# A sixth modulation unit folded by VectorE in the first FFN, and none left to the first attention

## The reference

```python
def adaln(cond, w, b):
    m = jax.nn.silu(cond) @ w + b
    return [t[:, None, :] for t in jnp.split(m, N_MOD, axis=-1)]

def ffn_sublayer(x, shift, scale, gate, g_pre, g_post, w_in, w_out):
    h = modulate(rmsnorm(x, g_pre), shift, scale)
    a, b = jnp.split(h @ w_in, 2, axis=-1)
    h = (jax.nn.silu(a) * b) @ w_out
    return x + FFN_RES * gate * rmsnorm(h, g_post)
```

## Time and profile before

| | |
|---|---|
| median of three runs | 3013.35 us (3012.11 to 3014.33) |
| the profiled execution's own time | 3015.84 us |
| its span | 3014.0 us, 46617 instructions |
| TensorE busy | 98% |
| VectorE busy | 73% |
| ScalarE busy | 38% |
| GpSimd busy | 19% |
| DMA | 517.76 MB, mean 172 GB/s |
| chain that ended last | TensorE 89% |

### The profile page before, as it was taken

One profiled execution on the slowest core, in us unless ns is written; L12 is line 12 of the kernel. 1 busy time (PEld: TensorE's weight loads), 2 busy tenths in 40 slices (PEclk: granted clock), 3 DMA queues, 4 the chain that ended last, 5 costly groups with the idle time before them and its releaser, 6 DMA issues.

```text
span 3014.0 us, 46617 instructions
## 1 busy us (share of the span) xinstructions
PE 2957.3 (98%) x18194; PEld 2748.1 (91%) x18194; DVE 2207.0 (73%) x2897; ACT 1153.1 (38%) x1966; POOL 564.2 (19%) x586
## 2 busy tenths in 40 slices
PE   7999999999999999999999999999999999999999
PEld 6999888999999998999899999979999999889998
DVE  6888678887987656888888576768888888775444
ACT  4222664223322424222422365543224222664222
POOL 1111212112111212111211144631112111211001
PEclk9999999999999999999999999999999999999999
DMA  8667436665665445766566443337665666333443
GB/s 299 210 213 216 146 84 193 211 211 170 215 213 175 116 131 173 226 211 197 185 214 192 134 118 105 97 95 236 211 209 184 216 211 200 108 81 113 127 128 96
DMA packets 589696, 517.76 MB, mean 172 GB/s; under 512 B 66773, under 2 KB 523046, under 8 KB 587686
## 3 DMA queue, kind: packets, MB, share of 16 engines
q1 hardware_dynamic: 588918, 514.53, 56.6%
q10 hardware_dynamic: 560, 0.25, 0.0%
HBM read 510.37 MB, written 4.33 MB: 171 GB/s over the span
## 4 chain that ended last, share of the span: by engine, by line
PE 89%; issue 4%; DVE 2%; POOL 2%; ACT 1%; DMA 1%; SPq 0%; another core or an unknown queue 0%; DVEq 0%; POOLq 0%; ACTq 0%
PE bank L1698 19%; PE bank L1700 18%; PE bank L1699 18%; PE bank L1749 9%; PE bank L1748 9%; PE bank L1747 9%; PE bank L1715 2%; PE bank L1722 1%; PE bank L619 1%; PE bank L644 1%; DMA ada_first<-w_ada 1%; PE bank L1780 0%; POOL small L2379 0%; POOL small L2384 0%; POOL hg_kr L1497 0%
## 5 line engine op out<-in xcount | busy, mean ns | idle before, releaser
L1698 PE MATMUL bank<-h_hi,w_hi 128*128 128x384 f32 x3328 | 1120.7, 337 | 0.0
L1700 PE MATMUL bank<-h_hi,w_lo 128*128 128x384 f32 x3328 | 1114.6, 335 | 0.0
L1699 PE MATMUL bank<-h_lo,w_hi 128*128 128x384 f32 x3328 | 1113.7, 335 | 0.0
L1934 ACT ACTIVATE w_hi<-raw 128x1024 fp32r<-128x1024 f32 x646 | 680.6, 1062 | 1022.8 <-PE bank L1700 481.8
L2090 DVE TENSOR_TENSOR w_lo<-raw,w_hi 128x1024 fp32r<-128x1024 f32 x648 | 811.1, 1275 | 310.6 <-ACT w_hi L1934 305.4
L1698 PEld LDWEIGHTS bank<-h_hi,w_hi 128*128 128x128 f32 x3328 | 625.3, 188 | 11.0 <-ACT tmp L1953 1.6
L1699 PEld LDWEIGHTS bank<-h_lo,w_hi 128*128 128x128 f32 x3328 | 625.4, 188 | 6.1
L1700 PEld LDWEIGHTS bank<-h_hi,w_lo 128*128 128x128 f32 x3328 | 625.1, 188 | 0.0
L2117 DVE SCALAR_TENSOR_TENSOR fold<-ada_raw,cond,fold 128x1024 f32<-128x1024 f32 x462 | 616.4, 1390 | 0.1
L2420 POOL TENSOR_TENSOR h_lo<-tmp,h_hi 128x384 fp32r<-128x384 f32 x176 | 249.3, 1416 | 1758.7 <-DVE h_hi L2161 1758.7
L1749 PE MATMUL bank<-w_hi,h_lo 128*128 128x512 f32 x1056 | 414.0, 392 | 0.0
(11 more groups left out here) (204 smaller groups left out, 2445.9 us busy)
## 6 DMA issues: line engine op xcount, KB each, us to landing
raw<-w_ffn_in SPq DMA_DIRECT2D x352, 512.0 KB, 5.0
ada_raw<-w_ada SPq DMA_DIRECT2D x264, 512.0 KB, 4.2
raw<-w_ffn_out SPq DMA_DIRECT2D x176, 512.0 KB, 4.7
raw<-w_hgrn_in SPq DMA_DIRECT2D x40, 512.0 KB, 4.1
g_rows<-g_dram SPq DMA_DIRECT2D x12, 1024.0 KB, 7.0
raw<-w_attn_qkv SPq DMA_DIRECT2D x24, 512.0 KB, 5.4
raw<-w_conv_in SPq DMA_DIRECT2D x24, 512.0 KB, 5.0
ada_first<-w_ada SPq DMA_DIRECT2D x16, 512.0 KB, 10.5
```

The lines of the kernel that those rows point to most:

```text
L1698: mm(out, wh, h_hi[:, k, :], start=(k == 0), stop=False)
L1699: mm(out, wh, h_lo[:, k, :], start=False, stop=False)
L1700: last = mm(out, wl, h_hi[:, k, :], start=False, stop=(k == DC - 1))
L1934: A(w_hi[:, b % RING, :], raw[:, b % RAW, :], ACT.Copy).then_inc(w_hi_made, 1)
```

## The change

The first FFN makes units 2 to 7, the first attention none. An FFN with up to five units keeps one in four iterations; the one with six has them start at f = 0, 4, 8, 11, 15, 18, so that three of them have three iterations, with three, three and two slabs. Their sums come at f = 4, 8, 11, 15, 18, 21, and the unit that is left over to the attention is unit 7 instead of unit 6. In SyncE's queue the slabs of the first FFN stand from block at_a(f) + 5 on, not + 3.

```diff
-    units_of = {0: (2, 7), 1: (7, 8), 2: (8, 13), 3: (13, 17), 4: (17, 17), 5: (17, 22), 6: (22, 26), 7: (26, 26),
+    units_of = {0: (2, 8), 1: (8, 8), 2: (8, 13), 3: (13, 17), 4: (17, 17), 5: (17, 22), 6: (22, 26), 7: (26, 26),
                 8: (26, 31), 9: (31, 36), 10: (36, 36), 11: (36, 36)}
     units_end = [units_of[s][1] for s in range(12)]
-    FOLD_F = 4
+    UNIT_STARTS = {5: (0, 4, 8, 12, 16, 20), 6: (0, 4, 8, 11, 15, 18, 21)}
+
+    def unit_starts(s):
+
+        u0, u1 = units_of[s]
+        return UNIT_STARTS[max(u1 - u0, 5)]
 
     def sums_of(s):
 
         u0, u1 = units_of[s]
-        return {FOLD_F * (u - u0 + 1): u for u in range(u0, u1)}
+        return {unit_starts(s)[u - u0 + 1]: u for u in range(u0, u1)}
...
-        u0, u1 = units_of[s]
-        u = u0 + f // FOLD_F
-        return [(u, 2 * (f % FOLD_F) + n) for n in range(2)] if u < u1 else []
+        starts = unit_starts(s)
+        for i, u in enumerate(range(*units_of[s])):
+            length = starts[i + 1] - starts[i]
+            if starts[i] <= f < starts[i + 1]:
+                per = -(-DC // length)
+                first = per * (f - starts[i])
+                return [(u, k) for k in range(first, min(first + per, DC))]
+        return []
...
-                        slabs.setdefault(at_a(f) + 3 + n, []).append(slab)
+                        slabs.setdefault(at_a(f) + (5 if s == 0 else 3) + n, []).append(slab)
```

## The result

The changed kernel took 3020.27 us in the median of 20 runs (3015.05 to 3026.24), the kernel before 3013.47 us beside it (20 runs, 3011.65 to 3017.41). The ratio, taken between runs made side by side, is 1.0018 with a 95% interval of 1.0012 to 1.0025, which is +5.4 us (+3.6 to +7.5). The forecast was −1.45 us, so it missed in size and in sign. The 3013.35 us that the forecast started from, plus 5.4, is 3018.8 us, above its range of 3008.7 to 3015.2. The profiled execution took 3020.82 us, with a span of 3019.0.

The account below looks back on a forecast made before the run. The prediction took TensorE, busy 98% of the span, as the bound. It summed −4.2 us in the attention and +2.75 us in the first FFN to −1.45 us, taking the median from 3013.35 to about 3011.9 us, range 3008.7 to 3015.2.

Parts of the forecast that it names:

- The attention, −4.2 us: First attention, up to its first scores: without its unit it takes the second attention's 21.76 us, saving 4.2 us.
- Steady part, three-slab iterations: First FFN, f = 8 to 19: VectorE lags 0.57 us, makes it up, and TensorE loses nothing.
- VectorE's work in the tail: End of first FFN: product 19 at 282.3, intervals 11.1 and 9.1 us, TensorE waits 2.0 us, boundary starts at 306.8.
- SyncE's queue … Cost nothing: First FFN's load queue: slabs loaded two blocks later still come ahead of their folds, at no cost.
- The term for the first FFN: End of first FFN: the added slabs and sums start VectorE's boundary chain late, +2.75 us.
- Rival D: First FFN's tail: last slab or unit 6's parts come late through SyncE's queue; +1.55 us, 3014.9; chance 0.08.
- The rule on the clock: First boundary: gaps between matmul bursts halve TensorE's clock, so the tail's new wait could add 1.7 us.
- rival C: First boundary gets a half-clock stretch, or another moves onto a boundary: +1.7 us, at most 3013.6; chance 0.13.
- a tail of 2.75 us: End of first FFN: the sixth unit's extra VectorE work delays the boundary by 2.75 us.

Follow-up runs that it names:

- packed version: Changed kernel with the first FFN's gains written as 128 rows of 64 bytes, layout left wrong: 3012.09 us, ratio 0.9994.
- second changed execution: The changed kernel profiled once more, unaltered: 3015.46 us.
- write from ScalarE: Changed kernel with the first FFN's scattered gains write issued from ScalarE's queue behind the Silu of f = 19: 3019.97 us, ratio 1.0018.
- write ahead of the slabs: Changed kernel with the first FFN's gains write directly behind block 63's load, before the two slabs there: 3018.65 us, ratio 1.0018.
- gains earlier: Changed kernel with the first FFN's gains write issued at block 61 instead of block 63: 3016.42 us, ratio 1.0008.
- third changed execution: The changed kernel profiled another time, unaltered: 3021.96 us.
- second of the kernel before: The kernel before the change profiled once more, unaltered: 3011.54 us.
- earlier starts: Changed kernel with the first FFN's units started at f = 0, 4, 7, 10, 13, 16 and ended at 19: 3010.37 us, ratio 0.9987.

## Why the prediction was wrong, point by point

- **The attention, −4.2 us: right.** The control in the same trace gave 21.76 us and 21.75 came; over three executions, taken from low parts to the next sublayer's low parts, the term is −3.7.
- **Steady part, three-slab iterations: right.** The lag was 0.4 us where I had 0.57, and it was made up.
- **VectorE's work in the tail: right.** Product 19 came at 282.15 (282.3). The packed version shows the intervals of 11.1 and 9.0 us, TensorE's wait of 2.0 us (in the changed kernel it does not come, since TensorE is held up earlier), and the boundary with next to no idle time (0.20 us).
- **"SyncE's queue … Cost nothing": this step failed.** I moved the slabs by two blocks and looked at what that does to slabs and weight loads in the steady part. I did not list what else stands in the queue at the last blocks. The write of the gains at block 63 was moved past by two slab loads, which wait for folds, so it left at 279.22 and not at 268.31, and the load behind it landed so late (15.3 us) that VectorE stood idle for 4.24 us. I had put the cost of moving the slabs at nothing; it measured 4.1 us. The term for the first FFN was +2.75 and measured +6.9 in the profile (310.83 − 304.07 = 6.76 at the boundary). It decides over the sign: −4.2 + 6.9 = +2.7. Of the +5.4 of the timed runs this leaves 2.7 us, which go with drops of the clock behind the first attention; whether the change causes these stays open.
- **Rival D was nearer than it looks.** It had the right place (SyncE's queue in the tail, slower) and expected the parts of unit 6's sums to come late. They did: the write of the sums took 12.3 us and not 4.5, its spreads left at 295.48, and VectorE, already 4.1 us late, still waited 0.34 us for them at 298.83. The forecast wanted them at 294.3, so by themselves they would have cost about 4.5 us (an estimate from these positions). But D's reason, the wait of SyncE for a landing of 4.5 us, was not it: the parts were a second victim of the gains' write. D also placed the last slab wrongly: f = 19's third and f = 20's first slab both stand at block 63, and the last one at block 64, ahead of block 65's load (286.26 and 286.63). The slab at 286.26 made nobody wait.
- **The rule on the clock, rival C.** A drop came with the new wait of 4.00 us (0.77 in 292 to 300), but it cost nothing there: TensorE was done with block b(21) when its next chunk began at 304.69, and VectorE started product 21 only at 306.58, without idle time, 9.04 us after product 20, as in the packed version, whose clock stood at 1.00 between these two products. So the chain was VectorE's. The second changed execution had a drop half as long in the tail (3.4 us in place of 6.8), and its first FFN was no shorter (+7.1, +6.9). Such a drop came in all five executions with a wait of 3.0 to 4.0 us of TensorE for product 20 (changed three times, write from ScalarE, write ahead of the slabs). In the packed version one came behind the wait of 2.0 us and cost about 0.5 us. With the gains written earlier, however, waits of 2.4 and 2.0 us left the clock at 1.00 (294 to 298; 298 to 306 likewise). So the rule of the Trainium skill that the prediction cites ("TensorE: Matmul & The Clock Gate", section "HAM oscillation — how this bites in real kernels") agrees with the traces of the changed and of the packed version and not with that of the gains earlier: a wait of about 2 us in the tail can bring the drop, and need not. A drop inside the first boundary, which is what C forecast, fell into the third changed execution and into the second of the kernel before, where there is no new wait; it cost 0.9 to 1.0 us each time, where C had 1.7.
- **That a tail of 2.75 us was the price of the sixth unit** was not necessary either: with earlier starts it is nothing, and in that profile the first two sublayers together are 5.8 us shorter than before (−3.9 us in the timed runs of the whole kernel).

## What to carry to other kernels

When instructions move in a queue, write down everything that stands at the places they are moved past, the small writes too, and ask for each what it does to the transfers behind it. In this kernel a write of 2048 single 4-byte elements belongs where no load that is needed soon is asked for in the next 8 to 10 us, or has to be packed; a kernel may contain such an empty place without a word on why. And extra work for an engine with spare time is best ended before the last iterations, because the tail has none of that spare time.

## What the runs showed of the hardware

- A write of 8 KB in 2048 elements of 4 bytes held up loads of 512 KB asked for within some 5 us behind it: 14.0 to 15.8 us to land, in seven executions of five versions, against 4.6 us behind the same 8 KB in rows of 64 bytes. Loads asked for 9 us behind it, before, took 8.0 us. The rate in between was 27 and 39 GB/s, against 192.
- It did so from ScalarE's queue as well (14.3 us). The write's small packets are begun early: in the kernel before 2112 packets under 512 bytes begin in the 5 us from its issue on and none in the 8.7 us behind that, and from 274 to 280 the busy share of the DMA engines is 0.01, yet the write has landed only at 283.13. So it is not that the engines are busy all the while; where the rest of the time goes, no run tells.
- In five executions of two nearly equal kernels TensorE's clock dropped to its lower level 4 to 9 times, mostly for 3.4 us. A drop added 0.9 to 1.4 us to a sublayer behind the attention, 0.9 to 1.0 us to the first boundary, and nothing in the tail where VectorE held the chain. A few more or fewer are as much as the whole effect studied here.
